# Differential attention with stationary values for two heads, and its norm taken over features

## What is computed

```python
s1 = einsum('bqhd,bkhd->bhqk', q1, k1) * scale
s2 = einsum('bqhd,bkhd->bhqk', q2, k2) * scale
amap = softmax(s1) - lam * softmax(s2)
o = einsum('bhqk,bkhd->bqhd', amap, v)
return rmsnorm(o, subln_w) * (1.0 - lambda_init)      # over the 64 features of a head
```

## Time and profile before

| | |
|---|---|
| median of 3 runs | 2196.41 us (2195.9 to 2201.15) |
| the profiled execution, its own time | 2195.54 us |
| its span | 2193.7 us |
| mean granted TensorE clock | 0.942 |
| TensorE busy | 1906.6 us, 87% |
| VectorE, ScalarE, GpSimd busy | 627.2, 504.4, 209.2 us |

### The profile page before, as it was taken

One profiled execution on the slowest core, in us unless ns is written; L12 is line 12 of the kernel. 1 busy time (PEld: TensorE's weight loads), 2 busy tenths in 40 slices (PEclk: granted clock), 3 DMA queues, 4 the chain that ended last, 5 costly groups with the idle time before them and its releaser, 6 DMA issues. The chain is left out here.

```text
span 2193.7 us, 25051 instructions
## 1 busy us (share of the span) xinstructions
PE 1906.6 (87%) x10554; PEld 915.5 (42%) x10554; DVE 627.2 (29%) x1168; ACT 504.4 (23%) x999; POOL 209.2 (10%) x225
## 2 busy tenths in 40 slices
PE   4998999979869999999996999999694978777775
PEld 2655565534423333333333766655341323222221
DVE  2257552362331111111105356523523100000002
ACT  3146541452200000000005145524221000000002
POOL 2300000110010111111101000001100100000000
PEclk9999999999879999999998999999796999888988
DMA  9520304112379999999999123014209999999997
GB/s 340 173 77 1 135 1 160 71 39 77 114 267 383 393 401 393 394 401 394 394 389 321 39 77 135 1 66 165 77 29 355 400 403 404 401 401 404 401 400 268
DMA packets 166368, 534.50 MB, mean 244 GB/s; under 512 B 10600, under 2 KB 19122, under 8 KB 166258
## 3 DMA queue, kind: packets, MB, share of 16 engines
q1 hardware_dynamic: 148112, 487.39, 57.1%
q0 software_dynamic: 16480, 40.21, 6.6%
q10 hardware_dynamic: 1666, 5.31, 0.6%
HBM read 507.72 MB, written 25.17 MB: 243 GB/s over the span
## 5 line engine op out<-in xcount | busy, mean ns | idle before, releaser
L2590 PE MATMUL ps<-ring,arena 128*64 128x512 f32 x1056 | 254.2, 635 | 47.1 <-DMA ring<-in_w_up 33.7
L2590 PE MATMUL ps<-arena 128*64 128x512 f32 x892 | 214.0, 629 | 30.8 <-DMA arena<-in_w_up 30.8
L1989 PE MATMUL ps<-arena,ring 128*128 128x256 f32 (+1 forms) x640 | 201.2, 476 | 9.6 <-DMA ring<-in_w_in 6.7
L2590 PEld LDWEIGHTS ps<-ring,arena 128*64 128x64 f32 x1056 | 81.7, 146 | 207.6 <-issue 204.0
L1989 PEld LDWEIGHTS ps<-arena,ring 128*128 128x128 f32 x640 | 122.6, 193 | 89.0 <-issue 69.6
L1908 DVE TENSOR_TENSOR arena<-arena,ps 128x512 f32<-128x512 f32 x32 | 22.0, 688 | 443.8 <-ACT arena L1241 443.8
L2498 PE MATMUL ps<-ring,arena 128*128 128x512 f32 x320 | 141.0, 594 | 0.4 <-DVE arena L1782 0.4
L2590 PEld LDWEIGHTS ps<-arena 128*64 128x64 f32 x892 | 69.8, 145 | 164.9 <-issue 164.9
L742 POOL DMA_INDIRECT expert_sums<-arena,small x32 | 51.6, 1613 | 857.1 <-ACT arena L1248 827.3
L2647 PE MATMUL ps<-ring,arena 128*64 128x512 f32 x544 | 122.6, 594 | 1.0 <-ACT arena L1255 0.7
L1241 ACT ACTIVATE arena<-ps 128x512 f32<-128x512 f32 x32 | 19.1, 597 | 439.2 <-PE ps L2590 439.2
(11 more groups left out here) (329 smaller groups left out, 2395.9 us busy)
## 6 DMA issues: line engine op xcount, KB each, us to landing
ring<-in_w_gate SPq DMA_DIRECT2D x35, 2048.0 KB, 21.5
ring<-in_w_down SPq DMA_DIRECT2D x34, 2048.0 KB, 22.4
ring<-in_w_up SPq DMA_DIRECT2D x31, 2048.0 KB, 15.8
arena<-in_w_down SPq DMA_DIRECT2D x25, 2048.0 KB, 23.7
ring<-in_ada_w SPq DMA_DIRECT2D x24, 2048.0 KB, 11.9
arena<-in_w_gate SPq DMA_DIRECT2D x24, 2048.0 KB, 21.0
arena<-in_w_up SPq DMA_DIRECT2D x23, 2048.0 KB, 15.3
ring<-in_w_in SPq DMA_DIRECT2D x6, 2048.0 KB, 13.0
```

Source lines behind the costliest of these rows:

```text
L1989: ins = mm(o[0:n, c0:c1], w[:, k, col:col + n], hT[:, k, c0:c1], start=k == 0, stop=k == KD - 1)
L2590: ins = mm(ps[0][hf * 64:hf * 64 + 64, col:col + 512], xl[e % 2][:, at:at + CAP_L], w[c][:, hf * 512:hf * 512 + 512], start=b + c == 0, st ...
```

## The change

- The units are renumbered: units 2i and 2i+1 are two heads of the same tile, so layer 0 has context units 0 to 3 and 12 to 15.
- Value products: the 128 x 64 values of each of the two heads are stationary and 128 columns of the turned map move; the heads write to PSUM partitions 0 to 63 and 64 to 127. The products of a pair are split over two iterations (half the keys in each), the last two pairs are done whole. The output comes feature by feature, in `mattT`. Turned maps have four buffers, not two.
- MLA's input projection is given to other iterations: layer 0 in iterations 2 to 6 and 12 to 17, layer 1 in 2 to 15.
- The outputs are not divided by the first map's sum. Instead the norm is taken of the raw outputs with eps times the square of that sum: TensorE sums the squares over the features with a 64 x 64 block of ones on each half of the partitions and adds the eps term by products of a spread column block with the identity (new job "on", two slots, before the queries). ScalarE takes Ln and Exp of the whole 128 x 512 or 128 x 768 result, twice, VectorE scales twice.
- The modulation columns are made among the products of the first query job and not of the second.
- The tail turns four blocks per tile and scales four.

```diff
-        for name, c in [..., ("datt", 4 * DH * q + 2),
-                        ("pre", 6), ("mq", 3), ("mrot", 2), ...
+        for name, c in [..., ("datt", len(diff_jobs(DH * q))),
+                        ("pre", 6), ("on", 2), ("mq", 3), ("mrot", 2), ...
+def values_after(u, n):
+    return [u - 1] if 2 <= u < n - 2 else [u] * (u == n - 2)
+def unit_tile(u, q):
+    return q[u // 2 % len(q)]
+def unit_head(u, q):
+    return u // 2 // len(q) * 2 + u % 2
 def latent_products(u, n):
-    share = {6: ((0, 4, 3, 1, 0, 0), (2, 3, 2, 1, 0, 0), (2, 3, 2, 1, 0, 0), (2, 2, 1, 1, 1, 1)),
-             4: ((0, 3, 3, 2), (2, 2, 2, 2), (2, 2, 2, 2), (2, 2, 2, 2))}[n // DH][h]
+    shares = {24: ((4, 4), (4, 3, 1), (2, 3, 3), (3, 3, 2)), 16: ((3, 3, 2), (2, 2, 2, 2), (2, 2, 2, 2), (3, 3, 2))}[n]
+    first = {24: (2, 4, 12, 15), 16: (2, 5, 9, 13)}[n]
...
 ACT, after the loop
-                act.wait_ge(*a.next(S["o_ss"]))
-                rsqrt(rstd[:, 4 * q[0]:4 * NT], ssum[:, 4 * q[0]:4 * NT], DV, S["o_rstd"])
                 turned_latents(2)
+                for p in range(2):
+                    j = jb("on") + p
+                    act.wait_ge(*J.filled(j))
+                    act.activation(orn[:, p, on], J.tile(j)[:, on], ACT.Ln, scale=1.0 / DV).then_inc(*J.free(j))
+                for p in range(2):
+                    act.wait_ge(*J.freed(jb("on") + p))
+                    act.activation(orn[:, p, on], orn[:, p, on], ACT.Exp, scale=-0.5).then_inc(S["o_rstd"], 1)
...
 DVE
+                    TT(s1sq[:, u:u + 1], esum[:, c:c + 1], esum[:, c:c + 1], ALU.mult)
...
-                dve.tensor_reduce(ssum[:, 4 * t0:4 * NT], ...)
-                for t in q:
-                    TT(o, o, rstd[:, 4 * t:4 * t + 4]...)
+                TT(osq[:, :, on], mattT[:, :, on], mattT[:, :, on], ALU.mult).then_inc(S["o_sq"], 1)
+                dve.tensor_scalar(view(s1b[:, 0:nu * DV], u=nu), s1sq[:, 0:nu]..., EPS * DV, None, ALU.mult).then_inc(S["o_sq"], 1)
...
+                for p in range(2):
+                    dve.wait_ge(*v.next(S["o_rstd"]))
+                    dve.scalar_tensor_tensor(mattT[:, p, on], orn[:, p, on], fac[:, 4 + p:5 + p], mattT[:, p, on], ...)
...
 PE
-                    for k in range(n):
-                        ins = mm(J.tile(j)[:, 0:DV], PT_d[u % 2][:, k * P:(k + 1) * P], V[:, k, h * DV:(h + 1) * DV], ...)
+                    k0 = n // 2 if u < nu - 2 else 0
+                    for k in range(k0) if u % 2 else range(k0, n):
+                        for b in range(2):
+                            h = unit_head(first + b, q)
+                            ins = mm(J.tile(j)[64 * b:64 * b + 64, 0:P], V[:, k, h * DV:(h + 1) * DV],
+                                     PT_d[(first + b) % 4][:, k * P:(k + 1) * P], ...)
...
+                pe.wait_ge(*w_.next(S["o_sq"], 2))
+                for p in range(2):
+                    j = jb("on") + p
+                    pe.wait_ge(*J.empty(j))
+                    for c0, c1 in ((t0 * P, 512), (512, TOK)):
+                        for r in (slice(0, 64), slice(64, P)):
+                            mm(J.tile(j)[r, c0:c1], K[r, K_ONE:K_ONE + 64], osq[r, p, c0:c1], start=True, stop=False)
+                    for i, t in enumerate(q):
+                        x = (p * nq + i) * P
+                        for b in range(2):
+                            ins = mm(J.tile(j)[64 * b:64 * b + 64, t * P:(t + 1) * P], s1b[:, x + 64 * b:x + 64 * b + 64],
+                                     ident, start=False, ...)
+                    ins.then_inc(*J.fill(j))
...
-                queries(jb("mq"), MH * MN)
-                queries(jb("mq") + 1, 0, (l, 1))
+                queries(jb("mq"), MH * MN, (l, 1))
+                queries(jb("mq") + 1, 0)
...
 def mixed(i):
-                              lambda k: Y[...] if k < 4 else matt[:, q[i], (k - 4) * P:(k - 3) * P], 6)
+                              lambda k: Y[:, q[i], k * P:(k + 1) * P], 4)
```

More of the change, by code:

```diff
@@ L971, in latents_out @@
                 def latents_out(t):
-                    home = J.tile(unit("value", 0))[:, 512:1024]
+                    home = J.tile(unit("value", 1))[:, 512:1024]
                     act.wait_ge(*a.next(S["mla_filled"]))
@@ L989, in _ @@
                         map_exps(u + 2)
[L990 to L993, removed]
+                    nk = n_keys(unit_tile(u, q))
+                    if u >= 4:
+                        act.wait_ge(*J.filled(unit("value", (u - 4) // 2 * 2 + 2)))
+                    copy_out(PT_d[u % 4][:, 0:nk], J.tile(unit("turn", u))[:, 0:nk], unit("turn", u))
                     lp = latent_products(u, nu)
@@ L1495, in _ @@
                         diff_weigh(u + 1)
-                    if u >= 1 and u < nu:
-                        diff_finish(u - 1)
+                    for n in values_after(u, nu):
+                        diff_finish(n)
                     for i in range(3):
@@ L1781, in mixed_out @@
                         dve.wait_ge(*J.filled(tail("out", i - 2)))
[L1782 to L1783 removed]
+                    TT(mixT[i % 2][:, 0:4, :], view(J.tile(j)[:, 0:4 * P], k=4),
+                       fac[:, 0:4].unsqueeze(2).to_broadcast([P, 4, P]), ALU.mult).then_inc(*J.free(j))
                 mixed_out(0)
@@ L2145, in diff_values @@
                 def diff_values(u):
-                    h, j, n = u // nq, unit("value", u), n_keys(q[u % nq]) // P
-                    pe.wait_ge(*J.freed(unit("turn", u)))
+                    first = u - 1 if u % 2 else u - 2
+                    j, n = unit("value", u), n_keys(unit_tile(first, q)) // P
+                    for x in (first, first + 1):
+                        pe.wait_ge(*J.freed(unit("turn", x)))
                     pe.wait_ge(*J.empty(j))
-                    for k in range(n):
-                        ins = mm(J.tile(j)[:, 0:DV], PT_d[u % 2][:, k * P:(k + 1) * P], V[:, k, h * DV:(h + 1) * DV],
-                                 start=k == 0, stop=k == n - 1)
+                    k0 = n // 2 if u < nu - 2 else 0
[3 more added lines that the diff above has]
+                            ins = mm(J.tile(j)[64 * b:64 * b + 64, 0:P], V[:, k, h * DV:(h + 1) * DV],
+                                     PT_d[(first + b) % 4][:, k * P:(k + 1) * P], start=k == 0, stop=k == n - 1)
                     ins.then_inc(*J.fill(j))
```

90 lines of the change are left out of this document (49 added, 41 removed).

## The result

| | before | after |
|---|---|---|
| median | 2197.60 us (4 runs, 2195.90 to 2201.15) | 2226.51 us (4 runs, 2223.40 to 2227.94) |
| span of the profiled execution | 2193.7 us | 2224.7 us |
| mean granted TensorE clock | 0.942 | 0.929 |
| TensorE, VectorE, ScalarE busy | 1906.6, 627.2, 504.4 us | 1927.5, 620.1, 508.6 us |

What follows compares the result with a forecast made beforehand. TensorE's path up to the router was taken as the bound, the differential loop closed by latency. Loops +0.5 and -2.0, norm +9.9, new wait +3.7, tail -2.8 gave +9.3 us: forecast 2205.5, range 2199 to 2213.

Steps and rivals of the forecast that it cites:

- The new wait: MLA's queries: the second query job waits for the column copy, TensorE idle 2.6 and 1.1 us; +3.7 (3.0 to 4.0).
- rival 2: Differential loop: the clock falls in the relieved iterations, period about 5.4 us in seven, +7, so 2212.5; chance 0.1.
- The norm: Before the queries: its new products add plain time on TensorE's path, 5.9 and 4.0 us; +9.9 (9.7 to 11.2).
- The loops: Differential loops: layer 0 +0.5 (-2 to +3), layer 1 -2.0 (0 to -3.6, by whether the starting lower clock lasts).
- the floor: Differential loop: latency from scores through maxima and exponentials keeps latent iterations 4.35 us apart, however little TensorE works.
- The tail: Tail: fewer turns per tile save 1.3 us, an earlier first projection 0.5 and 0.9; -2.8 (-2.2 to -3.2).
- 1: Norm: the two ones products, writing to one bank, don't run beside each other; +4.5, so 2210; chance 0.2.
- 3 (no floor): Differential loop: latency is no floor, all 19.1 us of relieved TensorE work comes through; -8.3, so 2188; chance 0.1.
- 4 (wait or norm covered): Queries and norm: unseen slack behind them covers the slot wait or the norm; -4, so 2201.5; chance 0.1.
- the scores are late by the lower clock again and again: Differential loop: a sign that would show the prediction wrong; no size given.

Runs made afterwards that it cites:

- experiment 1: The changed kernel with ScalarE copying out the modulation columns before the first query job instead of behind it: 2208.54 us, ratio 1.0051 to the kernel before.
- experiment 4: experiment 1 with the norm's products over the full 128 x 128 array instead of two 64 x 64 blocks: 2206.31 us, ratio 1.0042 to the kernel before.
- experiment 5: experiment 4 with the norm's squares, ones, spread columns and identity in bf16: 2203.18 us, ratio 1.0034 to the kernel before.
- experiment 6: experiment 1 with latent tiles before context tiles and MLA's input projection spread anew: 2199.43 us, ratio 1.0012 to the kernel before.
- experiment 8: experiment 1 with the norm of experiment 5 and the order of experiment 6: 2189.99 us, ratio 0.9976 to the kernel before.
- experiment 7: The kernel before with TensorE waiting for 8 tiny ScalarE copies in front of the state-space convolution: 2201.84 us, ratio 1.0027.
- experiment 9: The kernel before with TensorE waiting for 22 tiny ScalarE copies in front of the state-space convolution: 2205.04 us, ratio 1.0036.

## Why the prediction was wrong, step by step

**The new wait: the cause was right, its price was not.** The mechanism was as forecast to the instruction: the second query job waits for `columns_out` behind two copies, 2.32 and 0.83 us (forecast 2.6 and 1.1), 3.15 in all against +3.7. The step that failed is the price of this term: it counts the stop alone, and so leaves all queries, keys and values behind it at the durations that they had before. At 1.2 GHz the same work took 9.0 us more in layer 0 and 6.5 in layer 1. The term was 18.7 us, not 3.7, and these 15 us are some 70% of the miss of 21.0 us (2226.51 for 2205.5). I did ask where the clock would fall (rival 2), but only in the loop. That TensorE was now brought to a stop in a stretch where it had none (232.27 on the earlier trace rows) should have had the same question. The Trainium skill, "TensorE: Matmul & The Clock Gate", A second HAM failure mode: psum-queue depth-cycling, tells of short pauses of TensorE at PSUM slots which bring the clock down again and again. That is near to what the stretches above show, and I had not weighed it; that page has it for pauses in each iteration, here one was enough.

**The norm: right.** Forecast 5.9 and 4.0, measured 5.80 and 4.07 (1375.81 to 1379.88). ScalarE's and VectorE's part of it cost nothing: behind the first query the kernel of experiment 1 is as fast as the kernel before.

**The loops: right in layer 1, 1.7 us short in layer 0.** Layer 1: forecast -2.0, measured -2.5, of which 0.7 in nine steady iterations and the rest at the loop's start. Its steady iterations are at the floor (4.34, from 1320.08 to 1324.42), TensorE waits there for the exponentials:

```profile
1320.08 1.13 PE L2169 MATMUL ps<-arena,resid 32*128 32x512 f32 x8 [0.20 <-ACT arena L989]
...
1324.42 1.13 PE L2169 MATMUL ps<-arena,resid 32*128 32x512 f32 x8 [0.17 <-ACT arena L989]
```

The gain at the start hangs on the clock, as the term's range said: in experiments 4, 5, 6 and 8, where the lower clock ran for 10.2 us in this loop and not for 3.4, the loop took 69.45 to 69.46 us, 0.1 less than before.

Layer 0: latent iterations 4.34 us apart, with 1.60 us idle where there is no projection work (forecast some 1.8):

```profile
205.04 1.13 PE L2169 MATMUL ps<-arena,resid 32*128 32x512 f32 x8 [1.60 <-ACT arena L989]
...
206.91 0.88 PE L2186 MATMUL ps<-arena 128*64 128x128 f32 x12
209.38 1.13 PE L2169 MATMUL ps<-arena,resid 32*128 32x512 f32 x8 [1.60 <-ACT arena L989]
```

To the last scores +2.2 came for +1.8. The four context iterations in the middle took 14.7 us, not 12.4, part of them at the lower clock (in experiment 1, where it was up, 12.6), and the start took less than I gave it (9.9, not 12.2). Behind the last scores 1.3 us less was forecast and nothing came:

```profile
210.50:217.50 7.00, 6.42 (x35) 3.91 (x36) 4.58 (x9) 2.63 (x6) 0.00 (x0) 0.51 0.00 0
```

The clock was down there; in experiment 1, where it was up at that point, the same stretch took 10.1 instead of 11.1. A little of rival 2 is true, then: the relieved loop of layer 0 spent 17.1 us at the lower clock against 6.8. Against experiment 1, which spent 10.2 us there, that cost 1.2 us from the first scores to the turns (111.26 for 110.07), and not 7. The falls came at the context iterations and the end, not in the iterations that I had named. That a loop bound by latency hides most of the lower clock is my reading; no run tests it alone.

**The tail: turns and start right, the clock in layer 1 not.** Four turns take 0.43 us (530.40 to 530.83) for 0.66, and tiles that turn between projections are 0.22 us shorter each (8.03 from projection to projection, 8.25 before):

```profile
530.40 0.60 PE L2037 MATMUL ps<-const,arena 128*128 128x128 f32 x4
530.83 7.03 PE L2551 MATMUL ps<-ring,arena 128*128 128x512 f32 x16
```

The start came too. From the first turns to the first projection it was 1.92 us in layer 0 before (494.51 to 496.43) and is 1.44, and in layer 1 2.61 (1581.76 to 1584.37) and 1.90, so 0.5 and 0.7 less for 0.5 and 0.9. The table above has these in the row before the tail's. Before:

```profile
494.51 1.53 PE L2007 MATMUL ps<-const,arena 128*128 128x128 f32 x12
...
1581.76 2.82 PE L2007 MATMUL ps<-const,arena 128*128 128x128 f32 x12
1584.37 14.31 PE L2498 MATMUL ps<-ring,arena 128*128 128x512 f32 x32
```

After:

```profile
515.12 1.09 PE L2037 MATMUL ps<-const,arena 128*128 128x128 f32 x8
516.56 14.00 PE L2551 MATMUL ps<-ring,arena 128*128 128x512 f32 x32 [0.35 <-DVE arena L1812]
...
1610.86 1.97 PE L2037 MATMUL ps<-const,arena 128*128 128x128 f32 x8
1612.76 16.07 PE L2551 MATMUL ps<-ring,arena 128*128 128x512 f32 x32
```

But in layer 1 the first projection ran at the lower clock for longer and took 16.07 us instead of 14.31. From the first turns to the router's selection layer 0 is 2.0 us shorter and layer 1 0.7 longer, -1.3 in all for the -2.8 of the forecast. In experiment 1 it is -0.8 and -1.5, so -2.2.

**What no term had.** By its profile experiment 1 takes 9.6 us more than the kernel before (2203.3 for 2193.7), and the forecast without the new wait was +5.6. Its terms come to +5.9: the norm +9.7, the loops -1.5, the tail -2.2. The other 3.7 us lie in stages whose work the change left alone: 2.4 in layer 0's state-space stage, 1.6 in its experts, 0.8 behind layer 1's router, less 1.1 in front of the loop. In the state-space stage the lower clock ran for 17.1 us, where the kernel before has 10.2. That it is the cause was only argued, and so is whether another order of the work would move it.

**Sums of the forecast.** The tail's parts add up to 2.7, not 2.8. The median before plus the sum, 2196.4 + 9.3, is 2205.7, not 2205.5. The bounds of the loops and of the norm reach from -4.3 to +5.8 around the forecast where -2.6 to +5.5 is written. None of this changes the outcome: the measured time lies far outside all of them.

**Rivals.** 1 falls by experiment 4. 2 is true in its cause, wrong in place and size. 3 (no floor) falls: layer 0's loop took 1.1 us more with 7.3 us of work put back. 4 (wait or norm covered) falls by the 18.7 us and by the 9.7 of the norm, which experiment 1 keeps. The forecast "the scores are late by the lower clock again and again" as a sign against it didn't come; the queries were.

## What to carry to other kernels

When jobs are put into a ring of PSUM slots, look at every job behind them for the release that it now waits for, and order the releasing engine's copies so that the small one, which frees the slot, comes first. Price a new stop of TensorE not by its length alone but also with what stands behind it at half the clock: here a stop of 0.83 us cost 7.3. And ask of each relieved instruction whether it was in the ring that closes the loop; 19 us of work taken off TensorE gave nothing in one loop (2.2 us more) and 2.5 in the other.

## What the runs showed of the hardware

- The granted clock fell within or behind stops of 2.32 and 0.83 us in MLA's queries, and in one layer of one profile 2.2 us behind a stop of 0.29 us, and stayed at 1.2 GHz for 13.7 to 20.5 us, nearly all of it unbroken work. Stops of 1.39 us (experiment 7) and 2.69 us (experiment 9, layer 1) elsewhere left it at 2.4 GHz.
- Two fp32 products of 64 x 64 in opposite corners of the array, into the same bank, ran beside each other: 1.44 us for 512 + 256 columns in each half, against 1.40 for one product over the full array.
- In bf16 the norm's products took about 1.3 us (the work in front of them ends at 236.41, the queries start at 237.68; the first of them has no row of its own) for the 5.4 in fp32 (235.13 to 240.50).
